# Five of the seven norm reductions: seven adds on GpSimd and one product with ones, instead of eight products

## The reference, cut to what matters

```python
def rms_norm(x, g):
    x32 = x.astype(jnp.float32)
    y = x32 * lax.rsqrt(jnp.mean(x32 * x32, axis=-1, keepdims=True) + EPS)
    return (y * g.astype(jnp.float32)).astype(x.dtype)
...
    for l in range(DEPTH):
        h = rms_norm(x, norm_g[l])
...
        x = x + merged @ w_out[l]
    return rms_norm(x, final_g)
```

## Time and profile before

| what | value |
|---|---|
| median of 3 runs | 1518.5 us |
| profiled execution, first to last instruction (its span) | 1512.8 us |
| its own time as a run | not given apart from the span |
| TensorE busy | 1356.0 us (90%) in 12138 matmuls |
| VectorE busy | 860.9 us (57%) |
| ScalarE busy | 671.8 us (44%) |
| GpSimd busy | 265.1 us (18%) in 259 instructions |
| mean granted TensorE clock | 0.950 |

### The profile page before, as it was taken

The page is one execution under the profiler, slowest core; times in us unless marked ns, Lnnn a source line. Parts: engine busy times, 40 slices in busy tenths (PEclk is TensorE's granted clock), DMA queues, the critical chain, the costliest instruction groups (busy, mean ns, idle before and its releaser), DMA issues.

```text
span 1512.8 us, 32274 instructions
## 1 busy us (share of the span) xinstructions
PE 1356.0 (90%) x12138; PEld 1288.6 (85%) x12138; DVE 860.9 (57%) x1352; ACT 671.8 (44%) x1067; POOL 265.1 (18%) x259
## 2 busy tenths in 40 slices
PE   4889989979899989899658799999999899799997
PEld 4878978979799978898548789989989899799997
DVE  4334745546436645555488866666657565555544
ACT  5334435433434445433434553333333453566633
POOL 0000040006000220152042225336235000000000
PEclk9999989989999989999788999999999999999999
DMA  4524543334444523344223332231221454355553
GB/s 184 189 90 154 180 153 112 111 103 161 135 139 142 192 97 125 104 161 140 96 84 107 116 112 79 77 98 59 94 80 61 150 177 144 120 175 172 174 189 110
DMA packets 55481, 194.71 MB, mean 129 GB/s; under 512 B 6248, under 2 KB 9832, under 8 KB 54640
## 3 DMA queue, kind: packets, MB, share of 16 engines
q1 hardware_dynamic: 49248, 179.33, 36.1%
q10 hardware_dynamic: 5856, 13.30, 2.5%
q0 software_dynamic: 304, 1.07, 0.2%
HBM read 189.26 MB, written 4.41 MB: 128 GB/s over the span
## 4 chain that ended last, share of the span: by engine, by line
PE 61%; issue 22%; DVE 8%; ACT 3%; DVEq 2%; POOL 1%; POOLq 1%; DMA 1%; ACTq 0%
PE stream_ps L277 16%; PE stream_ps L279 15%; PE stream_ps L278 15%; DVE w_lo L269 2%; DVE qkvT L1099 2%; PE free_ps L1655 1%; PE free_ps L1638 1%; ACT w_hi L263 1%; PE free_ps L355 1%; PE free_ps L1656 1%; DVEq L1105 1%; POOLq L407 1%; PE free_ps L1403 1%; DMA cst<-cst_dram 1%; DVE oT L362 1%
## 5 line engine op out<-in xcount | busy, mean ns | idle before, releaser
L277 PE MATMUL stream_ps<-h_hi,w_hi 128*128 128x256 f32 (+1 forms) x2016 | 603.0, 299 | 54.8 <-DVE w_lo L269 25.6
L269 DVE TENSOR_TENSOR w_lo<-raw,w_hi 128x1024 fp32r<-128x1024 f32 x342 | 431.4, 1268 | 347.9 <-ACT w_hi L263 341.6
L279 PE MATMUL stream_ps<-h_hi,w_lo 128*128 128x256 f32 (+1 forms) x2016 | 585.6, 290 | 0.0
L278 PE MATMUL stream_ps<-h_lo,w_hi 128*128 128x256 f32 (+1 forms) x2016 | 585.5, 290 | 0.0
L277 PEld LDWEIGHTS stream_ps<-h_hi,w_hi 128*128 128x128 f32 x2016 | 393.4, 195 | 66.2 <-issue 31.9
L278 PEld LDWEIGHTS stream_ps<-h_lo,w_hi 128*128 128x128 f32 x2016 | 392.8, 195 | 0.7 <-issue 0.5
L279 PEld LDWEIGHTS stream_ps<-h_hi,w_lo 128*128 128x128 f32 x2016 | 392.7, 195 | 0.0
L263 ACT ACTIVATE w_hi<-raw 128x1024 fp32r<-128x1024 f32 x342 | 358.6, 1054 | 61.8 <-PE stream_ps L279 55.3
L1222 DVE TENSOR_TENSOR xy<-xy,free_ps 64x128 f32<-64x128 f32 x180 | 44.7, 283 | 62.7 <-PE free_ps L1656 47.4
L1099 DVE SCALAR_TENSOR_TENSOR qkvT<-st_raw,gains,qkvT 128x272 f32<-128x272 f32 x96 | 65.8, 726 | 5.3 <-ACT qkvT L681 2.6
L794 ACT ACTIVATE n<-free_ps 64x128 f32<-64x128 f32 x80 | 22.0, 275 | 105.2 <-PE free_ps L1638 104.3
(11 more groups left out here) (327 smaller groups left out, 2141.6 us busy)
## 6 DMA issues: line engine op xcount, KB each, us to landing
raw<-stream_dram SPq DMA_DIRECT2D x342, 512.0 KB, 3.5
gate_spill<-gate_out ACTq DMA_DIRECT2D x16, 136.0 KB, 2.0
xT<-xT_dram ACTq DMA_DIRECT2D x1, 1088.0 KB, 8.8
stage<-wik_dram ACTq DMA_DIRECT2D x2, 544.0 KB, 4.9
x_spill<-xT ACTq DMA_DIRECT2D x1, 1088.0 KB, 4.0
gb<-gate_spill ACTq DMA_DIRECT2D x1, 1088.0 KB, 7.0
ga<-gate_spill ACTq DMA_DIRECT2D x1, 1088.0 KB, 9.2
xT<-x_spill ACTq DMA_DIRECT2D x1, 1088.0 KB, 5.7
```

Of the source, the lines that this page charges most:

```text
L269: nc.vector.tensor_tensor(w_lo[s][:, :, :], raw[:, s, :].rearrange("p (k n) -> p k n", k=KT), w_hi[s][:, :, :].bitcast(F32), ALU.subtract) ...
L277: nc.tensor.matmul(ps, l_hi, r_hi, start=first, stop=False)
L278: nc.tensor.matmul(ps, l_hi, r_lo, start=False, stop=False)
L279: return nc.tensor.matmul(ps, l_lo, r_hi, start=False, stop=last)
```

## The change

`add_squares` on GpSimd adds tiles 1 to 7 of the squares to tile 0, one after another, each after a drain and a wait for that tile's square, and then signals `sqsum_ready`. `summed_squares` on TensorE waits for that and does one product with ones. Five sums are changed: the norm of layer 0, that of layer 1, the last norm of the first block (all 256 tokens), the norm ahead of the feed-forward part and the last norm of the kernel (272 tokens). The memory norm and the norm at the head of the second block keep the eight products.

```diff
@@ -355,6 +356,19 @@
                 mm = nc.tensor.matmul(free_ps[0][:, 0:n], ones, sq[:, k, :], start=k == 0, stop=k == KT - 1)
             mm.then_inc(ss_ready, 1)
 
+        def add_squares(pool, sq, sq_at):
+
+            for k in range(1, KT):
+                nc.gpsimd.drain()
+                pool.wait_ge(sq_ready, sq_at + k + 1)
+                op = nc.gpsimd.tensor_tensor(sq[:, 0, :], sq[:, 0, :], sq[:, k, :], ALU.add)
+            op.then_inc(sqsum_ready, 1)
+
+        def summed_squares(pe, sq, sums):
+
+            pe.wait_ge(sqsum_ready, sums)
+            nc.tensor.matmul(free_ps[0][:, 0:sq.shape[-1]], ones, sq[:, 0, :], start=True, stop=True).then_inc(ss_ready, 1)
+
...
             pool.sem_inc(part_used, 2)
+            add_squares(pool, wideS, 8)
             pool.wait_ge(flip_done, HEADS)
...
                     nc.gpsimd.drain()
-
+                add_squares(pool, wideS, 16 + 8 * l)
 
             pool.wait_ge(mlo_ready, 2 * LAYERS)
...
                     op.then_inc(sdec_ready, 1)
+            add_squares(pool, wide, 24 + 8 * LAYERS)
+            add_squares(pool, wide, 32 + 8 * LAYERS)
...
                 pe.wait_ge(pv_used, 6 * l + 1)
-                sum_squares(pe, wideS, 1 + l, 8 + 8 * l)
+                summed_squares(pe, wideS, l + 1)
...
-            sum_squares(pe, wideS, 1 + LAYERS, 8 + 8 * LAYERS)
+            summed_squares(pe, wideS, LAYERS + 1)
             sum_squares(pe, wide, 2 + LAYERS, 16 + 8 * LAYERS)
...
-            sum_squares(pe, wide, 3 + LAYERS, 24 + 8 * LAYERS)
+            summed_squares(pe, wide, LAYERS + 2)
...
-            sum_squares(pe, wide, 4 + LAYERS, 32 + 8 * LAYERS)
+            summed_squares(pe, wide, LAYERS + 3)
```

More of the change, by code:

```diff
@@ L213, in build @@
             sem(n) for n in ("sq_ready", "ss_ready", "rstd_ready", "n32_ready", "nhi_ready", "nlo_ready"))
+        sqsum_ready = sem("sqsum_ready")
         mem32_ready, memhi_ready, memlo_ready = (sem(n) for n in ("mem32_ready", "memhi_ready", "memlo_ready"))
```

## The result

The forecast was wrong. The changed kernel took 1536.1 us (median of four runs, 1531.2 to 1542.0) against 1518.1 us for the kernel before in the same comparison; the ratio is 1.0126, 95% interval 1.0095 to 1.0158. That is 18 us slower, where 1.1 us faster was forecast and 1520.6 us was the upper end of the range. The profiled execution took 1542.02 us as a run, 1.8 us more than its span; it was the slowest of the four, and its span is 27.4 us longer than that of the profile before.

The account below looks back on a forecast made before the run. TensorE's weight products were taken to bound the kernel (46% of the chain). Terms -1.44 - 1.16 + 0.77 + 0.86 - 0.63 + 0.55 = -1.05 us gave 1517.4 us, range 1514.8 to 1520.6 us.

Parts of the forecast that it names:

- Layer 0, layer 1, the first block's last norm, the feed-forward's, the last one: Five changed norms: Ln 1.44 and 1.16 us earlier, 0.77 and 0.86 us later, 0.63 us earlier, in that order.
- the guesses of the half clock for the single products: Products in layer 1's, the first block's last and the feed-forward norm: half clock after long idle, 1.22 or 1.27 us each.
- the middle: Kernel's last norm: product of 0.72 or 1.27 us, clock undecided after 2.2 us idle; midway gain of 0.63 us taken.
- The adds and their neighbours: GpSimd's adds in the 3.1 us rings: 0.73 to 0.77 us each, done before the next L269, costing nothing.
- the adds get in the way: Rival: GpSimd adds in the rings and last adds of three norms cost 4.2 us; 1521.6 us, chance 0.1.
- its add of 0.93 us: Add length in the rings from which the rival has GpSimd's add overlap and delay VectorE's L269.
- The restarts: TensorE's weight products behind the two layer norms: longer idle, so longer half clock, 0.55 us lost.
- the clock takes the gain back: Rival: both layer restarts at half clock for 5.8 us instead of 3.2, costing 2.6 us; 1519.5 us, chance 0.2.
- The 5.7 us: Whole kernel: the median lies 5.7 us above the profile's span, taken as unchanged.
- The change, norm by norm: Five changed norms: each gets one GpSimd add, one product and three hand-overs behind its last square, timed against the table load.

Follow-up runs that it names:

- e15: The kernel of e1 run again (changed kernel, step loop back in its place, no filling products); 1521.1 us, ratio 1.0028 to the kernel before.
- e1: The changed kernel with 64 semaphore increments on TensorE, putting the step loop's branch back at instruction 5093; 1520.4 us, ratio 1.0014 to the kernel before.
- e7: The kernel before, run once more without changes for a second profile; 1514.6 us.
- e2: The kernel before with 193 semaphore increments on TensorE ahead of the second block, moving the step loop's branch to 5285; 1545.3 us, ratio 1.0188.
- e4: Against the kernel before, only the norms of layers 0 and 1 and the last one changed, 36 increments keeping the loop's place; 1522.4 us, ratio 1.0029.
- e5: The changed kernel with products nobody reads in TensorE's idle time around the layer norms, 39 increments keeping the loop's place; 1514.2 us, ratio 0.9986.
- e13: The kernel before with unread products behind sums, 64 of 128 columns moving the loop one block, 4 of 512 at the feed-forward norm; 1512.4 us, ratio 0.9967.
- e10: The changed kernel, loop in place, with unread products around the norms, 4 of 512 columns behind each layer norm's sum; 1511.4 us, ratio 0.9952.
- e9: The changed kernel with 40 semaphore increments on TensorE, the step loop's branch at 5069; 1540.6 us, ratio 1.0140 to the kernel before.

## Why the prediction was wrong, point by point

- **Layer 0, layer 1, the first block's last norm, the feed-forward's, the last one.** Forecast -1.44, -1.16, +0.77, +0.86, -0.63; in the kernel after -1.48, -0.99, +0.83, +0.88, -0.88. These terms were right, and so were the guesses of the half clock for the single products. The last norm's product ran at full clock (0.72 us) behind 2.06 us of idle; I had taken the middle.
- **The adds and their neighbours.** Forecast 0.73 to 0.77 us and no effect; 0.72 to 0.79 us in the rings, which stayed at 3.1 us. The rival "the adds get in the way" is out: its add of 0.93 us did not occur there. Layer 0's seven adds took 7.5 us instead of some 6, for the two of 1.53 us, and were still long before they were needed. (The prediction says of its row that both engines read two operands; the copy in it reads one.)
- **The restarts.** The term was +0.55 us, drawn as a line through idle times, and it was mis-sized. With the loop in its place the kernel is 4.4 us slower than before (e15, 1521.1 against 1516.7; e1 gave 1.9), where the Ln alone give -1.6: the clock costs some 3.5 to 6 us. The forecast had this as the rival "the clock takes the gain back" at 1519.5 us and a chance of 0.2, too low in both. I looked at the first 5 us behind a restart and not at what runs next, the products of eight columns, during or behind which the clock falls a second time. And I had one profile of before, which happened to have no fall behind layer 0.
- **From span to median.** The 5.7 us were taken as what lies around the span. It is 1.8 us (e7: 1514.64 us as a run, 1512.8 us span); the rest is that the profiled execution was faster than the median. The forecast is a difference, so nothing hung on it.
- **The step that failed.** "The change, norm by norm" costed what the change removes at the products' own durations, and the sum had no term for anything outside the norms, their restarts and the adds' neighbours. The 63 instructions that leave TensorE's program ahead of the step loop were put at nothing without a word. They move a loop that had run without fetches to a place where it stalls at each jump back. This costs 14.3 us by the steps of the loop in the profile; by the medians, each against its own kernel before, it is 13.6 us (18.0 less e15's 4.4) to 16.1 us (less e1's 1.9). That is about three quarters of the miss of 18.7 us. It was to be seen: from 949 to 1139 us the instruction queue brings nothing in the kernel before, so the loop lives on what is held. The two programs side by side gave the count of instructions that moved.

The memory stage's +3 us in the profile after is not the change's: e2, with norms that nobody changed, has +2.7 us at the same place, and e4, e5 and e15, with changed norms, have none.

## What to carry to other kernels

An edit that adds or removes instructions moves all that comes after it. Where a long loop runs without instruction fetches, count how far the edit shifts it and look at the instruction queue and at "issue" idle at the jump before and after; if the loop has slipped, restore its place first, and only then judge the edit. Second, TensorE's work in a wait isn't always waste: with one product in place of eight the half clock behind it lasted longer, and this gave back more than the change won; with other products in the idle time the kernel came out 0.5% under the one before. Third, extra semaphore increments are a good tool for moving code but cost 0.1 us each; in e13 64 filling products moved the loop by 256 as well, and the kernel stayed under the one before.

## What the runs showed of the hardware that I had not expected

- A loop of 1773 TensorE instructions costs nothing for fetches at one place, and at another a stall of 2.7 to 4.5 us at each jump back and in most rounds a stretch at half clock behind it, together 3 to 7 us a round. Moves by +23, -24 and -63 instructions made it slow, one by +256 did not.
- A semaphore increment on TensorE takes 0.1 us (100 of them 9.6 us).
- The granted clock can fall from full to half during or just behind 32 rows of float32 products of eight columns (3.6 us of work), even when TensorE had been busy but for 0.58 us; it did so behind both layers in e13, and did not in e10.
- A drain on GpSimd waited for a transfer that its own queue had issued. GpSimd's first add in the changed kernel came after 9.6 us of idle that the timeline gives to nobody ("issue"). The drain ahead of it stands in the trace from 34.65 to 44.98 us; the load of `hankel` was issued at 34.60 and landed at 44.84. In e1, e9 and e15 too the drain ended 0.14 us behind that landing. It is hidden here, but it would not be in a kernel whose first add is on the path. The timeline, then the drains of L362 (shortest, median and longest in ns), then the load (KB, us to landing):

```profile
34.60 0.95 POOL L404 DMA_DIRECT2D hankel<-rel_scratch  x1 [1.55 <-DMA rel_scratch<-rel_f]
45.16 7.54 POOL L364 TENSOR_TENSOR wide<-wide 128x256 f32<-128x256 f32 x7 [9.61 <-issue]
```

```profile
L362 POOLq DRAIN  x7: 797/829/10328, 34.6 to 51.1; - x7
hankel<-rel_scratch POOLq DMA_DIRECT2D x1, 1024.0 KB, 10.2
```
